# First unit of products between the token turns, memsets and small copies moved, at the beginning of a hybrid decoder step

## The chip, the cores and the metric

One Trainium2 chip, one of its cores. The metric is the time of one execution on the device in microseconds. The engines are TensorE (PE, matmul; PEld is its weight load), VectorE (DVE), ScalarE (ACT), GpSimd (POOL) and SyncE (SP), which issues most DMAs. TensorE's clock has two levels, 1.2 and 2.4 GHz; the profile writes the granted clock as a share of full speed.

## The reference, cut to what matters

One layer of a decoder trunk for 512 prompt tokens and 32 sample tokens, 544 columns in all, width 1024. Every sub-layer has an RMSNorm in front and behind. The change touches the beginning of the first sub-layer:

```python
hp = rms_norm(y_p, g_mix_pre[l])          # x * rsqrt(mean(x^2) + eps) * g
proj = hn @ w_in                          # 1024 -> 2048: q, k, v (512 each), u (512)
# S5 on u: diagonal complex scan, 32 groups of 16 channels, 64 states each
dt = jnp.exp(log_dt)[:, None]
lam_bar = jnp.exp(lam * dt)
b_bar = ((lam_bar - 1.0) / lam)[..., None] * lax.complex(b_re, b_im)
bu = jnp.einsum("btgh,gph->btgp", uf, b_bar)
_, h = lax.associative_scan(combine, (a, bu), axis=1)
y = jnp.real(jnp.einsum("btgp,ghp->btgh", h, c)) + d_skip * uf
```

Behind it come differential attention, a GLU, an output projection, a cross-attention into 256 memory tokens and a SwiGLU FFN. They are not changed.

## The kernel before

Every large product is made in three parts of reduced precision: weights and activations are split into a high part (`w_hi`, `x_hi`, a rounding copy on ACT) and a low part (`w_lo`, `x_lo`, a subtraction on DVE or POOL), and PE adds hi x hi, hi x lo and lo x hi in PSUM. Features lie on the partitions, the 544 token columns are two halves of 272. Weights come in units of 1 MB (`w_raw`, two slots; 8 feature tiles x 256 columns): SP loads unit n when `w_lo` of unit n-2 is made, ACT makes `w_hi` (L702), DVE makes `w_lo` (`split_lo`, L1141). Unit n gives the output tiles j = 2n and 2n+1, each 8 x 3 x 2 = 48 matmuls (L1806 in `product`). The accumulator of tile j is a pair of banks that depends on j mod 2 (`acc`), so `product` waits with `acc_out >= j - 1` until tile j-2 has been moved out by ACT.

The beginning, line by line. SP loads the tokens (`x_nat`), `ident`, `ones` (L466), the first weight unit and the parameters of the scan. POOL zeroes `c_out` and `c_pad`, waits for the scaled tokens, and zeroes `b_pad` (L634). ACT and DVE take the sums of squares, the roots, and scale the tokens into `xs` (L794, L1195). PE turns the rows of small parameters and of `log_dt` (L1843); DVE copies the first into `par`, halves four columns of it (L1199) and copies the second (L1202). ACT makes `w_hi` of unit 0. PE then turns the tokens, feature tile by feature tile: five transposes a tile (L1862, four of 128 tokens and one of 32) into the banks `X_BANKS`; ACT makes `x_hi` (L799) and DVE `x_lo` (L1206) of each tile, straight from PSUM.

After that every engine walks the same hand-written list `order` and does its share of each entry, in its own queue. Its start is `par, main 0, mats_c, main 1, mats_b 0, main 2, mats_b 1, main 3, fir, main 4, s5s 0`.

- `par`: the scan's parameters. ACT: exponential of dt (L820), `w_hi` of unit 1 (`hi_ahead(1)`), exponential of the two `lam_dots` (L823), and once DVE has the arguments (`p_arg`), tanh and two sines (L825 to L827, a table load between them). DVE: `lam_dots` (L1241), the lambda scalars, the arguments (to L1268), `split_lo` of unit 1, and with the sines a long row of small operations (from L1272), `split_lo` of unit 2 (44.57 us in the rows below), the copies of the turned `c` into `c_pad` and `c_sgn` (L1340, L1341), and `b_pad`.
- `main n`: PE multiplies unit n; ACT moves its two tiles out (units 0 and 1 into `uT`, L811) and makes `w_hi` of unit n+2.
- `mats_c`: PE turns the start states and `c` (10 transposes); DVE makes `split_lo` of unit 3, `c_out`, and zeroes `fir` (L1396).
- `mats_b n`: PE turns one of the two matrices of `b_pad`, 16 transposes; the first has `keep_busy(bank(4), 10)` in front, matmuls on `ident` without a use (L1830), two per call. The second waits for all four copies of the first (`bT_out`). ACT copies them into `b_in` (L832). DVE makes `rot` and two low parts.

In ACT's queue `par` thus stands ahead of the evacuation of unit 0, and PE's second unit waits for that evacuation:

```python
            if first and j >= 2:
                e.wait_ge(acc_out, j - 1)
```

Of the kernel before, what the change touches and what calls it, by code (L numbers as in the profile page):

```python
# [80 lines left out]
def build(nc, A, O):  # L81
# [79 lines left out]
    b_pad = at("b_pad", [P, 2, CH, SF, P], F32, C0 + 8704)  # L161
    st_nat = at("st_nat", [P, 2, P], F32, C0 + 27648)
# [5 lines left out]
    x_nat = at("x_nat", [P, 5, D], F32, C0)  # L168
# [197 lines left out]
    X_BANKS = (4, 6, 2, 0, 4, 6, 4, 6)  # L366
# [10 lines left out]
    order = [("par", 0), ("main", 0), ("mats_c", 0), ("main", 1), ("mats_b", 0), ("main", 2), ("mats_b", 1), ("main", 3),  # L377
# [69 lines left out]
    def _(sp_eng):  # L447
# [16 lines left out]
        e.dma_start(x_nat[0:NS_TOK, 4, :], A["x_sample"].rearrange("b t d -> (b t) d")).then_inc(x_in, 16)  # L464
# [155 lines left out]
    def _(pool):  # L620
# [64 lines left out]
    def _(act):  # L685
# [95 lines left out]
        e.wait_ge(S("eps_ready"), 1)  # L781
        e.activation(small[:, 60:61], small[:, EPS_COL:EPS_COL + 1], ACT.Sqrt)
        for t in SQ_ACT:
            rows = P if t < 4 else NS_TOK
            e.wait_ge(*((S(f"x_in{t}"), 16) if t < 4 else (x_in, 16)))
            e.activation(xs[0:rows, t, :], x_nat[0:rows, t, :], ACT.Square, accum_out=small[0:rows, t:t + 1]).then_inc(S("x_ss"), 1)
        e.wait_ge(S("x_ms"), 2)
# [14 lines left out]
        for kind, n in order:  # L802
            if kind == "m7":
                evac(14 + n, two(vT[:, 2 + n, :]))
            elif kind == "main":
# [10 lines left out]
                hi_ahead(min(n + 2, U_GLU))  # L816
            elif kind == "par":
# [3 lines left out]
                hi_ahead(1)  # L821
# [5 lines left out]
                e.activation(sp[:, 6], sp[:, 3], ACT.Sin, scale=0.5).then_inc(S("p_funcs"), 1)  # L827
            elif kind == "mats_b":

                for d in range(CH):  # L830
                    e.wait_ge(S("bT_full"), CH * n + d + 1)
                    e.activation(b_in[:, :, n, d, :], bank(4 + d).rearrange("p (a b) -> p a b", a=SF), ACT.Copy)\  # L832
                        .then_inc(S("bT_out"), 1)
            elif kind == "fir":
                e.wait_ge(S("fir_full"), 1)
# [93 lines left out]
            elif kind == "mem_a":  # L929
# [4 lines left out]
                e.wait_ge(S("x_ms"), 2 + 1)  # L934
# [189 lines left out]
    def _(dve):  # L1124
# [54 lines left out]
        e.memset(small[:, EPS_COL:EPS_COL + 1], EPS).then_inc(S("eps_ready"), 1)  # L1179
# [7 lines left out]
        e.tensor_scalar(small[:, 8:12], small[:, 0:4], 1.0 / D, EPS, ALU.mult, ALU.add).then_inc(S("x_ms"), 1)  # L1187
        e.tensor_scalar(small[0:NS_TOK, 12:13], small[0:NS_TOK, 4:5], 1.0 / D, EPS, ALU.mult, ALU.add).then_inc(S("x_ms"), 1)
# [47 lines left out]
        for kind, n in order:  # L1236
            if kind == "par":
# [31 lines left out]
                split_lo()  # L1269
# [1111 lines left out]
```

## Time and profile before

| what | us |
|---|---|
| median of three runs (all: 981.1, 981.74, 985.83) | 981.74 |
| the profiled execution, its own time | 980.58 |
| its span, first to last instruction | 978.8 |
| PE busy in the span | 934.9 |
| DVE, ACT, POOL busy | 438.3, 357.2, 198.8 |
| mean granted clock of TensorE | 0.992 |

Read the start first: the list of slices of the page shows PE at three tenths in the first fortieth of the span (24.5 us) and at nine tenths from the second on. The busy share says nothing of the speed: the matmuls of the first unit are busy at a lower clock as well. Times in the rows are microseconds from the start of the span; a row of the timeline merges like instructions and gives the start of the first, the time from there to the end of the last, and how many there are.

### The profile page before, as it was taken

The page shows a single profiled execution, that of the slowest core. Times are in us where ns is not written, and L with a number is a line of the kernel's source. Part 1 is how long each engine was busy: PE and PEld are TensorE (multiplying, and loading weights), DVE is VectorE, ACT ScalarE, POOL GpSimd, SP SyncE. Part 2 cuts the span into 40 slices and gives each one's busy share as a digit, 9 for nine tenths or more (in the row PEclk, how much of TensorE's full clock was granted, in tenths as well). Part 3 has the DMA queues.
Part 4 walks back from the last instruction along what each step waited for, and adds up shares of the span by engine and source line. Part 5 has one row for each costly group of instructions (what it writes and reads, how often), then busy time and mean ns, then how long its engine had stood idle before and what let it go on. Part 6 is the DMA issues. An engine that isn't in the chain of part 4 may idle for free.

```text
span 978.8 us, 17712 instructions
## 1 busy us (share of the span) xinstructions
PE 934.9 (96%) x7526; PEld 863.0 (88%) x7526; DVE 438.3 (45%) x876; ACT 357.2 (36%) x560; POOL 198.8 (20%) x66
## 2 busy tenths in 40 slices
PE   3999999889899999999989999999999999999997
PEld 2999998765799889976569899999999999999996
DVE  5799974565445696121644662222222222001103
ACT  5432223665454473145425542222222222222111
POOL 3000000202100033200110003333333333343330
PEclk9999999999999999999999989999999999999999
DMA  7314205432342359268142011222222222222212
GB/s 209 110 40 131 85 4 191 149 116 87 117 148 64 112 181 330 90 249 310 40 133 86 2 44 47 92 93 92 93 94 90 86 86 75 87 76 76 86 33 92
DMA packets 81247, 105.84 MB, mean 108 GB/s; under 512 B 9473, under 2 KB 64642, under 8 KB 81058
## 3 DMA queue, kind: packets, MB, share of 16 engines
q1 hardware_dynamic: 80960, 104.92, 32.3%
q8 instruction: 46, 0.75, 0.3%
q14 instruction: 15, 0.12, 0.0%
q10 hardware_dynamic: 226, 0.05, 0.0%
HBM read 98.26 MB, written 6.70 MB: 107 GB/s over the span
## 4 chain that ended last, share of the span: by engine, by line
PE 87%; DVE 5%; ACT 4%; issue 2%; DMA 1%; ACTq 0%; DVEq 0%; POOL 0%
PE pall L1806 59%; PE pall L1818 7%; PE pall L2128 4%; PE pall L1843 3%; PE pall L2179 1%; PE pall L1830 1%; PE pall L2198 1%; PE pall L2004 1%; PE pall L1879 1%; PE pall L2234 1%; PE pall L1996 1%; PE pall L1896 1%; PE pall L1862 1%; PE pall L1900 1%; DVE a_s L1464 1%
## 5 line engine op out<-in xcount | busy, mean ns | idle before, releaser
L628 POOL TENSOR_TENSOR w_lo<-w_raw,w_hi 128x2048 fp32r<-128x2048 f32 (+1 forms) x38 | 170.3, 4483 | 462.4 <-ACT w_hi L702 380.3
L1806 PE MATMUL pall<-x_hi,w_hi 128*128 128x272 f32 x1024 | 214.0, 291 | 0.5 <-issue 0.5
L1806 PE MATMUL pall<-x_lo,w_hi 128*128 128x272 f32 x1024 | 212.6, 289 | 0.0
L1806 PE MATMUL pall<-x_hi,w_lo 128*128 128x272 f32 x1024 | 211.2, 288 | 0.0
L1806 PEld LDWEIGHTS pall<-x_hi,w_hi 128*128 128x128 f32 x1024 | 161.0, 189 | 1.4 <-issue 0.7
L1806 PEld LDWEIGHTS pall<-x_lo,w_hi 128*128 128x128 f32 x1024 | 162.0, 190 | 0.0
L1806 PEld LDWEIGHTS pall<-x_hi,w_lo 128*128 128x128 f32 x1024 | 161.2, 189 | 0.0
L702 ACT ACTIVATE w_hi<-w_raw 128x2048 fp32r<-128x2048 f32 (+1 forms) x61 | 114.9, 1883 | 106.6 <-PE pall L1806 91.9
L1806 PE MATMUL pall<-g_hi,w_hi 128*128 128x272 f32 x352 | 73.2, 289 | 0.0
L1806 PE MATMUL pall<-g_lo,w_hi 128*128 128x272 f32 x352 | 72.8, 288 | 0.0
L1806 PE MATMUL pall<-g_hi,w_lo 128*128 128x272 f32 x352 | 72.7, 288 | 0.0
L1141 DVE TENSOR_TENSOR w_lo<-w_raw,w_hi 128x2048 fp32r<-128x2048 f32 x23 | 52.7, 2290 | 10.8 <-ACT w_hi L702 10.7
L1135 DVE TENSOR_TENSOR sq<-pall,rstd 128x544 f32<-128x544 f32 (+1 forms) x24 | 16.3, 677 | 91.7 <-PE pall L1806 87.8
L1806 PEld LDWEIGHTS pall<-g_lo,w_hi 128*128 128x128 f32 x352 | 55.4, 189 | 0.0
L1806 PEld LDWEIGHTS pall<-g_hi,w_hi 128*128 128x128 f32 x352 | 55.2, 189 | 0.0
L1806 PEld LDWEIGHTS pall<-g_hi,w_lo 128*128 128x128 f32 x352 | 55.1, 189 | 0.0
L1135 DVE TENSOR_TENSOR tt<-pall,rstd 128x544 f32<-128x544 f32 (+1 forms) x24 | 16.1, 676 | 83.6 <-PE pall L1806 80.4
L1103 ACT ACTIVATE g_hi<-sq 128x544 f32 x20 | 13.2, 659 | 98.1 <-DVE sq L1135 98.1
L1138 DVE TENSOR_TENSOR sqacc<-sqacc,sq 128x544 f32<-128x544 f32 x12 | 11.3, 941 | 76.3 <-ACT sq L735 76.3
L1099 ACT ACTIVATE tt<-tt 128x544 f32<-128x544 f32 x20 | 13.2, 659 | 79.3 <-DVE tt L1135 79.3
L1818 PE MATMUL pall<-x_hi,w_hi 128*128 128x272 f32 x128 | 37.4, 292 | 0.7 <-DVE x_lo L1141 0.7
L1818 PE MATMUL pall<-x_hi,w_lo 128*128 128x272 f32 x128 | 37.0, 289 | 0.0
(383 smaller groups left out, 1582.5 us busy)
## 6 DMA issues: line engine op xcount, KB each, us to landing
w_raw<-in_w_gate SPq DMA_DIRECT2D x10, 1024.0 KB, 5.3
w_raw<-in_w_up SPq DMA_DIRECT2D x10, 1024.0 KB, 5.3
w_raw<-in_w_in SPq DMA_DIRECT2D x8, 1024.0 KB, 6.9
w_raw<-in_w_down SPq DMA_DIRECT2D x8, 1024.0 KB, 5.2
dm_kv<-in_cache_mem_v SPq DMA_DIRECT2D x5, 1024.0 KB, 13.8
w_raw<-in_w_out SPq DMA_DIRECT2D x4, 1024.0 KB, 8.3
d_k<-in_cache_k SPq DMA_DIRECT2D x16, 256.0 KB, 3.3
d_v<-in_cache_v SPq DMA_DIRECT2D x16, 256.0 KB, 4.2
```

Source lines behind the costliest of these rows:

```text
L628: e.tensor_tensor(w_lo[:, n % 2, 0:w], w_raw[:, n % 2, 0:w], w_hi[:, n % 2, 0:w].bitcast(F32), ALU.subtract)\
L702: e.activation(w_hi[:, n % 2, 0:w], w_raw[:, n % 2, 0:w], ACT.Copy).then_inc(w_hi_ready, 1)
L1099: e.activation(tt[:, m, :], tt[:, m, :], ACT.Silu).then_inc(S("silu"), 1)
L1103: e.activation(g_hi[:, bass.ds(i * 2 + (m + 2), 1), :], sq[:, m:m + 1, :], ACT.Copy).then_inc(S("g_hi_ready"), 1)
L1135: return e.tensor_tensor(out, a, b, ALU.mult)
L1138: return e.tensor_tensor(out, a, b, ALU.add)
L1141: return e.tensor_tensor(out, a, b, ALU.subtract)
L1464: ins = e.tensor_tensor_reduce(out=a_s[:, n % 2, c, 0:nk], in0=bank(c)[:, 0:nk], in1=alibi[:, h, ALIBI_W - nk:ALIBI_W], scale=1.0, scalar=NEG,
L1806: ins = mm(acc(j)[:, a, :], w, x[:, k_x + k, a * HALF:(a + 1) * HALF], start=first and k == 0 and s_, stop=last and k == kts - 1 and t_)
L1818: ins = mm(out[:, 0:HALF], w, x[:, k, in_half(a)], start=k == 0 and s_, stop=k == KT - 1 and t_)
L1843: ins = e.transpose(dst[0:src.shape[1], at_:at_ + w], src, ident[0:w, 0:w])
L2128: ins = mm(bank(2 * (pr % 2) + t), x[:, 4 * part + k, rows], w[:, n % 2, w_cols], start=part == 0 and k == 0 and i == 0, stop=part == 1 an ...
```

## The change

The tokens of the samples get a tile of their own (`xs_nat`), so that `b_pad` and `st_nat` can lie elsewhere; `b_pad` is zeroed right behind `c_out`, `c_pad` after three low parts. PE runs `keep_busy` twice before the first turn. `w_hi` and `w_lo` of unit 0 are made in two halves, the second halves between the tiles 1 and 2 of the tokens. The eight turns of tokens use two pairs of banks in alternation; from the third on a turn stands between the products of the tiles before (`first_unit`). `w_hi` of unit 1 is made before tile 6 of `x_hi`; `split_lo` of unit 1 goes from the middle of `par` to right behind the last low part of the tokens. The copies into `c_pad` and `c_sgn` and the zeroing of `fir` go from DVE to ACT. `mats_b 0` stands behind main 2, directly in front of `mats_b 1`, whose banks now wait one by one; `w_hi` of unit 4 is made behind it. Some semaphores are merged (`eps_ready` and `x_ms` into `x_eps_ms`).

```diff
     st = at("st", [P, 2, P], F32, C0 + 94208)
-    b_pad = at("b_pad", [P, 2, CH, SF, P], F32, C0 + 8704)
-    st_nat = at("st_nat", [P, 2, P], F32, C0 + 27648)
+    b_pad = at("b_pad", [P, 2, CH, SF, P], F32, C0 + 19968)
+    st_nat = at("st_nat", [P, 2, P], F32, C0 + 17408)
     st_end = [at("st_end0", [P, P], F32, C0 + 95232), at("st_end1", [P, P], F32, Y0 + 16896)]
...
-    x_nat = at("x_nat", [P, 5, D], F32, C0)
+    x_nat = at("x_nat", [P, 4, D], F32, C0)
+    xs_nat = at("xs_nat", [P, D], F32, TMP)
     xs = at("xs", [P, 5, D], F32, C0 + 45056)
...
     XS_ACT, XS_DVE = (0, 4), (1, 2, 3)
-    X_BANKS = (4, 6, 2, 0, 4, 6, 4, 6)
-    order = [("par", 0), ("main", 0), ("mats_c", 0), ("main", 1), ("mats_b", 0), ("main", 2), ("mats_b", 1), ("main", 3),
+    X_BANKS = (4, 6) * (KT // 2)
+    order = [("par", 0), ("main", 0), ("mats_c", 0), ("main", 1), ("main", 2), ("mats_b", 0), ("mats_b", 1), ("main", 3),
              ("fir", 0), ("main", 4), ("s5s", 0), ("main", 5), ("s5s", 1), ("main", 6), ("s5y", 0), ("s5s", 2), ("m7", 0),
...
         e.memset(c_out[:], 0.0).then_inc(S("zeroed"), 1)
+        e.memset(b_pad[:], 0.0).then_inc(S("zeroed"), 1)
+        e.wait_ge(S("xs_lo"), 3)
         e.memset(c_pad[:], 0.0).then_inc(S("zeroed"), 1)
-        e.wait_ge(S("xs_ready"), 5)
-        e.memset(b_pad[:], 0.0).then_inc(S("zeroed"), 1)
         e.wait_ge(S("s5_y"), SF)
...
             rows = P if t < 4 else NS_TOK
-        hi_ahead(0)
+        def first_hi(half):
+            cols = slice(half * 1024, (half + 1) * 1024)
+            ins = e.activation(w_hi[:, 0, cols], w_raw[:, 0, cols], ACT.Copy)
+            ins.then_inc(w_hi_ready, 1) if half else ins.then_inc(S("xs_hi"), 1)
+        e.wait_ge(w_loaded[0], 16)
+        todo[0] = 1
+        first_hi(0)
         e.wait_ge(S("par_ready"), 1)
         for k in range(KT):
+            if k == 2:
+                first_hi(1)
+            elif k == 6:
+                hi_ahead(1)
             e.wait_ge(S("xsT_full"), k + 1)
...
                     evac(j, two(dst[:, t, :]), scale=HD ** -0.5 if dst is qT else 1.0)
-                hi_ahead(min(n + 2, U_GLU))
+                if n != 2:
+                    hi_ahead(min(n + 2, U_GLU))
             elif kind == "par":
...
                 e.activation(sp[:, 1], sp[:, 0], ACT.Exp).then_inc(S("p_funcs"), 1)
-                hi_ahead(1)
                 e.wait_ge(S("lam_dots"), 2)
...
                 e.activation(sp[:, 6], sp[:, 3], ACT.Sin, scale=0.5).then_inc(S("p_funcs"), 1)
+            elif kind == "mats_c":
+                e.wait_ge(S("zeroed"), 3)
+                for r in range(2):
+                    e.wait_ge(S("cT_full"), r + 1)
+                    for d in range(2):
+                        rows = slice(64 * d, 64 * d + 64)
+                        src = bank(4 + r)[rows, :].rearrange("p (f d h) -> p f d h", d=2, h=GH)[:, :, d, :]
+                        e.activation(c_pad[rows, :, r, 16 * d:16 * d + 16], src, ACT.Copy, scale=1.0 - 2.0 * r).then_inc(S("cT_out"), 1)
+                        e.activation(c_sgn[rows, r], src, ACT.Copy, scale=1.0 - 2.0 * r).then_inc(S("cT_out"), 1)
             elif kind == "mats_b":
...
                         .then_inc(S("bT_out"), 1)
+                if n:
+                    hi_ahead(4)
             elif kind == "fir":
+                e.wait_ge(S("c_out"), 4)
+                e.activation(fir[:].rearrange("p a b c -> p (a b) c"), ident[:].unsqueeze(1).broadcast_to([P, SF * CH, P]), ACT.Copy, scale=0.0)\
+                    .then_inc(S("fir_zero"), 1)
                 e.wait_ge(S("fir_full"), 1)
...
         e.tensor_copy(sp[:, 0], bank(2)[:, 0:CT_N]).then_inc(S("dtT_ready"), 1)
-        split_lo()
+        def first_lo(half):
+            e.wait_ge(*((w_hi_ready, 1) if half else (S("xs_hi"), 1)))
+            cols = slice(half * 1024, (half + 1) * 1024)
+            ins = sub(w_lo[:, 0, cols], w_raw[:, 0, cols], w_hi[:, 0, cols].bitcast(F32))
+            if half:
+                ins.then_inc(w_lo_ready, 1)
+        lo_done[0] = 1
+        first_lo(0)
         for k in range(KT):
-            e.wait_ge(S("xs_hi"), k + 1)
+            if k == 2:
+                first_lo(1)
+            e.wait_ge(S("xs_hi"), k + 2)
             e.scalar_tensor_tensor(out=x_lo[:, k, :], in0=banks(X_BANKS[k]), scalar=par[:, G_MIX_PRE + k:G_MIX_PRE + k + 1],
                                    in1=x_hi[:, k, :].bitcast(F32), op0=ALU.mult, op1=ALU.subtract).then_inc(S("xs_lo"), 1)
+        split_lo()
...
                 e.tensor_scalar(c(3), c(7), 3.1415925, -3.1415925, ALU.min, ALU.max).then_inc(S("p_arg"), 1)
-                split_lo()
                 e.wait_ge(S("p_funcs"), 2 + 3)
...
                 e.tensor_copy(st[:].rearrange("p a b -> p (a b)"), bank(6)[:, 0:2 * P]).then_inc(S("st_ready"), 1)
-                for r in range(2):
-                    e.wait_ge(S("cT_full"), r + 1)
-                    if r == 0:
-                        e.wait_ge(S("zeroed"), 2)
-                    for d in range(2):
-                        rows = slice(64 * d, 64 * d + 64)
-                        src = bank(4 + r)[rows, :].rearrange("p (f d h) -> p f d h", d=2, h=GH)[:, :, d, :]
-                        e.tensor_scalar(c_pad[rows, :, r, 16 * d:16 * d + 16], src, 1.0 - 2.0 * r, None, ALU.mult).then_inc(S("cT_out"), 1)
-                        e.tensor_scalar(c_sgn[rows, r], src, 1.0 - 2.0 * r, None, ALU.mult).then_inc(S("cT_out"), 1)
...
                         e.tensor_tensor(c_out[rows, :, r, :, 16 * g:16 * g + 16], t0[rows], t1[rows], op).then_inc(S("c_out"), 1)
-                e.wait_ge(S("c_out"), 4)
-                e.memset(fir[:], 0.0).then_inc(S("fir_zero"), 1)
             elif kind == "fir":
...
         e.wait_ge(consts_in, 32)
+        keep_busy(bank(6), 12)
         e.wait_ge(rows_in, 16 * N_ROW_LOADS)
...
         transposes(bank(2), [dt_rows[:].rearrange("p a b -> p (a b)")]).then_inc(S("dtT"), 1)
-        for k in range(KT):
-            if k == 0:
-                e.wait_ge(S("xs_ready"), 5)
-            if k in (2, 3):
-                e.wait_ge(*((S("par_ready"), 1) if k == 3 else (S("dtT_ready"), 1)))
-            if k >= 4:
-                e.wait_ge(S("xs_lo"), (1, 2, 5, 6)[k - 4])
+        keep_busy(bank(6), 8)
+        e.wait_ge(S("xs_ready"), 5)
+        def x_turn(k):
+            if k >= 2:
+                e.wait_ge(S("xs_lo"), k - 1)
             for t in range(5):
...
             ins.then_inc(S("xsT_full"), 1)
+        def first_product(m, k):
+            e.wait_ge(S("xs_lo"), k + 1)
+            if k == 4:
+                e.wait_ge(w_lo_ready, 1)
+            wcol = slice(k * 256 + m * P, k * 256 + (m + 1) * P)
+            wh, wl = w_hi[:, 0, wcol], w_lo[:, 0, wcol]
+            for w, x, s_, t_ in ((wh, x_hi, True, False), (wh, x_lo, False, False), (wl, x_hi, False, True)):
+                for a in range(2):
+                    ins = mm(acc(m)[:, a, :], w, x[:, k, a * HALF:(a + 1) * HALF], start=k == 0 and s_, stop=k == KT - 1 and t_)
+            return ins
+        def first_unit():
+            e.wait_ge(S("dtT_ready"), 1)
+            for k in range(KT - 2):
+                e.wait_ge(S("xs_lo"), k + 1)
+                x_turn(k + 2)
+                for m in range(2):
+                    first_product(m, k)
+            for m in range(2):
+                for k in (KT - 2, KT - 1):
+                    ins = first_product(m, k)
+                ins.then_inc(acc_full, 1)
+        x_turn(0)
+        x_turn(1)
...
             if kind == "main":
-                unit(n, J_W_IN + 2 * n, KT, 256, x_hi, x_lo, ready=(lambda k: (S("xs_lo"), max(4, k + 1))) if n == 0 else None)
+                if n == 0:
+                    first_unit()
+                else:
+                    unit(n, J_W_IN + 2 * n, KT, 256, x_hi, x_lo)
             elif kind == "m7":
...
                 e.wait_ge(S("st_ready"), 1)
-                if n:
-                    e.wait_ge(S("bT_out"), CH)
-                else:
+                if n == 0:
                     keep_busy(bank(4), 10)
...
                 for d in range(CH):
+                    if n:
+                        e.wait_ge(S("bT_out"), d + 1)
                     transposes(bank(4 + d), [b_pad[:, n, d, f, :] for f in range(SF)]).then_inc(S("bT_full"), 1)
```

## Rows read from the trace of the kernel before

**Rows 1.** Page, part 1: busy us of each engine, share, instructions

```profile
PE 934.9 (96%) x7526; PEld 863.0 (88%) x7526; DVE 438.3 (45%) x876; ACT 357.2 (36%) x560; POOL 198.8 (20%) x66
```

**Rows 2.** Chain of waits, 0 to 200 us: start us, us, what

```profile
14.48 3.50 DVE par L1199
...
22.03 0.72 ACT x_hi L799
22.77 0.80 DVE x_lo L1206
...
26.26 14.12 PE pall L1806 x96
40.37 1.09 PE pall L1843 x10
41.46 12.04 PE pall L1806 x96
53.50 2.23 PE pall L1830 x20
```

**Rows 3.** Timeline, 0 to 62 us: start us, us, engine line op, what, count

```profile
3.64 0.45 SPq L466 DMA_DIRECT2D ones<-in_t_ones  x1
...
14.44 3.52 POOL L634 MEMSET b_pad<- 128x4096 f32 x1 [9.30 <-ACT xs L794]
...
29.98 0.62 PE L1806 MATMUL pall<-x_hi,w_lo 128*128 128x272 f32 x2
...
30.43 0.41 PE L1806 MATMUL pall<-x_hi,w_hi 128*128 128x272 f32 x2
...
30.68 0.42 PE L1806 MATMUL pall<-x_lo,w_hi 128*128 128x272 f32 x2
```

**Rows 4.** Timeline of PE, 11 to 27 us

```profile
18.06 5.22 PE L1862 MATMUL pall<-ident,xs 128*128 128x128 f32 x20 [0.98 <-DVE sp L1202]
```

**Rows 5.** DMA issues, 0 to 12 us: count, KB, us to landing

```profile
ones<-in_t_ones SPq DMA_DIRECT2D x1, 64.0 KB, 6.9
```

**Rows 6.** Timeline of PE, 286 to 300 us, turns at 2.4 GHz

```profile
294.28 0.77 PE L1970 MATMUL pall<-ident,x_res 128*128 128x128 f32 x5
294.98 0.66 PE L1843 MATMUL pall<-ident,mem_nat 128*128 128x128 f32 x4
```

**Rows 7.** Timeline, 0 to 62 us, the parameters of the scan

```profile
27.74 0.22 DVE L1241 CUSTOM_DVE_ANT_0 lamp<-lamv 128x64 f32<-128x64 f32 x1
...
30.24 0.19 ACT L823 ACTIVATE small<-small 128x2 f32<-128x2 f32 x1
...
30.46 0.16 DVE L1141 TENSOR_TENSOR small<-small 128x1 f32<-128x1 f32 x1 [2.30 <-ACT small L823]
...
32.71 0.17 DVE L1268 TENSOR_SCALAR sp<-sp 128x16 f32<-128x16 f32 x1
32.79 2.29 DVE L1141 TENSOR_TENSOR w_lo<-w_raw,w_hi 128x2048 fp32r<-128x2048 f32 x1
...
34.67 1.18 ACT L811 ACTIVATE uT<-pall 128x544 f32<-128x544 f32 x1
...
35.00 0.17 DVE L1272 TENSOR_SCALAR sp<-sp 128x16 f32<-128x16 f32 x1
```

**Rows 8.** Timeline of PE at 196 us, then stretches: busy us, clock, DMA, GB/s

```profile
196.27 2.43 PE L2101 MATMUL pall<-ident,small 68*128 68x68 f32 x16 [2.43 <-DVE small L1533]
...
198.00:199.00 1.00, 1.00 (x7) 1.00 (x7) 0.00 (x0) 0.00 (x0) 0.00 (x0) 0.50 0.96 345
559.00:560.00 1.00, 0.68 (x3) 0.69 (x4) 1.00 (x4) 1.00 (x3) 0.00 (x0) 0.75 0.00 0
568.00:569.00 1.00, 1.00 (x6) 1.00 (x6) 1.00 (x4) 0.84 (x2) 0.00 (x0) 0.50 0.00 0
```

**Rows 9.** Timeline of DVE, 36 to 75 us

```profile
44.57 2.29 DVE L1141 TENSOR_TENSOR w_lo<-w_raw,w_hi 128x2048 fp32r<-128x2048 f32 x1
...
72.51 1.76 DVE L1396 MEMSET fir<- 128x2048 f32 x1 [0.49 <-DVE c_out L1394]
```

More of the change, by code:

```diff
@@ L463, in _ @@
             e.dma_start(x_nat[:, t, :], x_view[:, t, :]).then_inc(S(f"x_in{t}"), 16)
-        e.dma_start(x_nat[0:NS_TOK, 4, :], A["x_sample"].rearrange("b t d -> (b t) d")).then_inc(x_in, 16)
+        e.dma_start(xs_nat[0:NS_TOK, :], A["x_sample"].rearrange("b t d -> (b t) d")).then_inc(x_in, 16)
         e.dma_start(ident[:], A["t_ident"]).then_inc(consts_in, 16)
@@ L780, in _ @@
         e.dma_start(dt2[:], A["ssm_log_dt"][0].rearrange("(c g) -> c g", g=2)).then_inc(rows_in, 16)
-        e.wait_ge(S("eps_ready"), 1)
+        e.wait_ge(S("x_eps_ms"), 1)
         e.activation(small[:, 60:61], small[:, EPS_COL:EPS_COL + 1], ACT.Sqrt)
@@ L785, in _ @@
             e.wait_ge(*((S(f"x_in{t}"), 16) if t < 4 else (x_in, 16)))
-            e.activation(xs[0:rows, t, :], x_nat[0:rows, t, :], ACT.Square, accum_out=small[0:rows, t:t + 1]).then_inc(S("x_ss"), 1)
-        e.wait_ge(S("x_ms"), 2)
+            e.activation(xs[0:rows, t, :], x_nat[:, t, :] if t < 4 else xs_nat[0:rows, :], ACT.Square, accum_out=small[0:rows, t:t + 1]).then_inc(S("x_ss"), 1)
+        e.wait_ge(S("x_eps_ms"), 3)
         e.activation(small[:, 8:12], small[:, 8:12], ACT.Sqrt)
@@ L793, in _ @@
             rows = P if t < 4 else NS_TOK
-            e.activation(xs[0:rows, t, :], x_nat[0:rows, t, :], ACT.Copy, scale=small[0:rows, 16 + t:17 + t]).then_inc(S("xs_ready"), 1)
-        hi_ahead(0)
+            e.activation(xs[0:rows, t, :], x_nat[:, t, :] if t < 4 else xs_nat[0:rows, :], ACT.Copy, scale=small[0:rows, 16 + t:17 + t])\
+                .then_inc(S("xs_ready"), 1)
+        def first_hi(half):
[5 more added lines that the diff above has]
+        first_hi(0)
         e.wait_ge(S("par_ready"), 1)
         for k in range(KT):
+            if k == 2:
+                first_hi(1)
+            elif k == 6:
+                hi_ahead(1)
             e.wait_ge(S("xsT_full"), k + 1)
@@ L933, in _ @@
                     e.activation(mem_sq[:, t, :], mem_nat[:, t, :], ACT.Square, accum_out=small[:, t:t + 1]).then_inc(S("x_ss"), 1)
-                e.wait_ge(S("x_ms"), 2 + 1)
+                e.wait_ge(S("x_eps_ms"), 3 + 1)
                 e.activation(small[:, 8:10], small[:, 8:10], ACT.Sqrt).then_inc(S("x_root"), 1)
@@ L1177, in split_lo @@
             lo_done[0] += 1
-        e.memset(small[:, EPS_COL:EPS_COL + 1], EPS).then_inc(S("eps_ready"), 1)
+        e.memset(small[:, EPS_COL:EPS_COL + 1], EPS).then_inc(S("x_eps_ms"), 1)
         for t in SQ_DVE:
@@ L1186, in _ @@
         e.wait_ge(S("x_ss"), 5)
-        e.tensor_scalar(small[:, 8:12], small[:, 0:4], 1.0 / D, EPS, ALU.mult, ALU.add).then_inc(S("x_ms"), 1)
-        e.tensor_scalar(small[0:NS_TOK, 12:13], small[0:NS_TOK, 4:5], 1.0 / D, EPS, ALU.mult, ALU.add).then_inc(S("x_ms"), 1)
+        e.tensor_scalar(small[:, 8:12], small[:, 0:4], 1.0 / D, EPS, ALU.mult, ALU.add).then_inc(S("x_eps_ms"), 1)
+        e.tensor_scalar(small[0:NS_TOK, 12:13], small[0:NS_TOK, 4:5], 1.0 / D, EPS, ALU.mult, ALU.add).then_inc(S("x_eps_ms"), 1)
         e.wait_ge(S("x_root"), 1)
@@ L1542, in _ @@
                 e.wait_ge(S("x_ss"), 5 + 2)
-                e.tensor_scalar(small[:, 8:10], small[:, 0:2], 1.0 / D, EPS, ALU.mult, ALU.add).then_inc(S("x_ms"), 1)
+                e.tensor_scalar(small[:, 8:10], small[:, 0:2], 1.0 / D, EPS, ALU.mult, ALU.add).then_inc(S("x_eps_ms"), 1)
                 e.wait_ge(S("x_root"), 1 + 1)
```

## The prediction

> **What bounds the kernel now.** I read the page first: TensorE (PE) is busy for 934.9 us of a span of 978.8 us [rows 1]. Only what moves PE's queue of work can change the time, so the next view is the chain of waits over the start [rows 2]. It shows 3.50 us in which `par` on VectorE (DVE) alone is what everybody waits for, then the token turns, and from 26.26 us on PE without a break: the first unit of products (14.12 us for 96 matmuls), the ten turns of `mats_c` at 40.37, and the second unit at 41.46 us (12.04 us for as many). From there PE goes on through `keep_busy` (53.50) and the later units. I therefore measure the change at one point: **when the second unit starts, 41.46 us now**. The order `mats_b` moves in is neutral for PE if nobody is late, so whatever is won or lost there reaches the end.
>
> The all-engine timeline shows two reasons for the slow start [rows 3]. `par` on DVE takes 3.50 us for four columns, and it starts and ends with GpSimd's (POOL's) memset of `b_pad` (14.44 to 17.96 us). And the products run at two speeds: from 29.98 to 30.43 us is 0.45 us a pair, from 30.43 to 30.68 it is 0.25 us. The first spacing is 272 columns each at 1.2 GHz, the second belongs to 2.4 GHz; the clock rose at about 30.3 us. 20 turns in 5.22 us [rows 4] are part of the eight microseconds of turns before the products, which had not raised it; the products had run 4.0 us when it rose.
>
> **The change, part by part.**
>
> *Memsets.* `b_pad` is zeroed right behind `c_out`, a tile of the same size: two times 3.52 us from 0.7 us on, until 7.8 us, when DVE waits for tokens anyway. `par` then costs what its neighbours of this size do, about 0.2 us, and 3.3 us go from the chain. The Trainium skill (SBUF — State Buffer, "Who interferes with whom") says that GpSimd and a VectorE instruction that uses both ports exclude each other for a whole instruction; by that rule, too, the wait is gone, and the `c_pad` memset, now behind three low parts, could hold DVE up once more. It has a quarter of `b_pad`'s columns, so 0.9 us at most, between two low parts that PE wants 2.2 us apart: I take 0, and 0.9 as the upper end.
>
> *Warming.* Ten `keep_busy` calls are 20 matmuls in 2.23 us, 0.111 us each at 2.4 GHz [rows 2]; at 1.2 GHz I take twice that, 0.22 us. The 12 + 8 calls are 40 matmuls: 4.5 us if all warm, 8.9 us if none. They can start when `ones` has landed, 3.64 [rows 3] + 6.9 = 10.5 us [rows 5]. With the clock rising 4.0 us after, as now: 18 matmuls at 0.22 (to 14.5), 6 at 0.111, the two parameter turns (0.3), 16 at 0.111: 17.2 us. The bounds are 15.3 (all warm) and 20.0 us (none).
>
> *First unit between the turns.* A warm turn of one feature tile takes 0.70 us (294.28 to 294.98) [rows 6]. Turns 0 and 1 end at 17.9 and 18.6; `x_hi` 0.72 and `x_lo` 0.80 [rows 2] put the first low part at P0 = 19.4 us. Then six steps of one turn and twelve matmuls, 0.70 + 12 x 0.125 (12.04 us / 96) = 2.20 us, and 3.0 us for the last two tiles: the unit ends at P0 + 16.2 = 35.6 us and `mats_c` at 36.7, against 41.46. **On PE that is 4.8 us won.** The half-unit splits on ScalarE (ACT) and DVE are the same columns in two pieces and lie beside PE. `w_hi` of unit 1, before tile 6, is covered: tile 6 is turned only four steps after P0.
>
> *What is behind it in the queues.* The second unit may not overwrite the first accumulator before ACT has moved it to `uT`. In ACT's queue that evacuation stands behind `par`: exponentials, tanh, sines, each waiting for DVE. Now this is over in time [rows 7]: `lam_dots` on DVE at 27.74, exponential on ACT, arguments 30.46 to 32.88, table load and sines, `uT` 34.67 to 35.85, 5.6 us before PE wants it. In the changed kernel DVE's low parts are stretched over the unit, and `split_lo` of unit 1 has been put between the last low part and `lam_dots`. The last low part is at T7 = P0 + 5 x 2.20 + 0.70 + 0.72 + 0.80 = 32.6 us. Behind it: `w_lo` 2.29, `lam_dots` 0.35 (two like 0.22, one behind the other), exponential and its hand-over 0.2, arguments 2.42, from there to the end of `uT` 2.97 (32.88 to 35.85): 8.25 us. **The second unit starts at 32.6 + 8.25 = 40.9 us**, not 36.7. The win of 4.8 us shrinks to 0.6, with PE idle for 4.2 us.
>
> *The clock in that gap.* The rows for a fallen clock [rows 8]: after 2.43 us idle before 196.27 the clock was 0.50 in 198 to 199; and it was low from 559 to 569 us, 10 us long, where PE had had some gaps of up to 1 us. So 4.2 us idle most probably costs a new rise, 4.0 us at half speed = 2.0 us lost; ends 0 (it holds) and 5 us (as at 559). I take 2.0, by the one rise under products. The Trainium skill (TensorE: Matmul & The Clock Gate, "Why this matters for your kernels") says that idle gaps between bursts of matmuls put the engine back to its low clock; the fall at 196 us agrees, and by the rule rival 1 below has little.
>
> *Moved from DVE to ACT.* Eight small copies for `c_pad` and `c_sgn`, and the zeroing of `fir` (1.76 us on DVE) [rows 9]. On ACT the copies stand between `w_hi` of unit 2 and the next evacuation, the zeroing behind main 3, where the unit's 12 us hold only about 5 us of ACT's work. If that cover were gone they would cost their own length, some 4 and 2 us; here 0. DVE's later work is not late: behind the sines it has 9.6 us to its next `w_lo` (35.00 to 44.57) [rows 7, 9], so `w_lo` of unit 2 is ready near 39.7 + 9.6 + 2.3 = 51.6 us, and main 2 wants it at 53 or later. 1.3 us of slack, tied to the same event.
>
> *`mats_b` behind the third unit.* The same 20 + 32 instructions. In the second matrix each bank waits for its own copy on ACT, which began with the first bank of the first matrix, while PE was at its other three: 0, and at most the last copy's half microsecond. `w_hi` of unit 4 stands behind both and is wanted only after main 3.
>
> Sum: -0.6 + 2.0 = **+1.4 us**, so 980.58 + 1.4 = 982.0 us for the profiled execution; the median of the runs shown stands 1.2 us above that execution, so I forecast 983.2 us.
>
> **Rivals.**
> 1. *The same wait, but the clock holds through the gap.* For it: gaps of about 1 us in the token stage don't count here, and PE comes out of 20 dense microseconds. Against: 2.43 us was enough at 196. 981.74 - 0.6 = 981.1 us.
> 2. *The win is kept.* ACT's `par` part is done sooner than I add up, and the second unit starts at 36.7: 981.74 - 4.8 = 977.0 us. Against it is the order of the two queues in the diff; the chain would have to shrink from 8.25 to 4 us.
> 3. *The low clock through the start (slower).* The place is the stretch from 10.5 us to T7, and what decides is P0: the second unit starts at P0 + 21.45, so above P0 = 20.0 us the change loses, one for one. If the 40 warming matmuls all run at 1.2 GHz, they and the parameter turns end at 20.0, turns take 1.29 us [rows 4], P0 = 22.8; one first step at 1.2 GHz (1.29 + 2.72 = 4.0 us), the rest warm: 37.8 = T7, 46.1 us for the second unit, +4.6, and +2.0 behind the gap: 988.3 us. If the clock stays down through the unit, T7 is 45.6 and the sum +14, 996 us. For it: the eight microseconds of turns that did not raise it, and 559 to 569. Against: `keep_busy` is matmuls, not turns. The Trainium skill (TensorE: Matmul & The Clock Gate, "Part 4: PE-mode transpose") says that a transpose doesn't count as TensorE being busy in the same way; the low stretch from 18.06 us agrees, and mixing turns into the unit speaks against this change by it.
> 4. *The change does not do what it says*, that is, the products don't run between the turns: the loop is written out, I give it nothing of its own.
>
> **How the numbers follow.** Forecast 0.48 (981.5 to 984.5, up to 987 with a long low clock), rival 1 0.20 (980 to 982), rival 2 0.09 (976.5 to 978.5), rival 3 0.23 (985 to 996, most of it under 990). The three runs before spread from 981.1 to 985.83 us, so about 0.5% is what a measurement can tell from no change: 976.8 to 986.6. The range from 979.5 to 989.5 leaves out rival 2 and the far half of rival 3. Faster by over 0.5% needs more than the whole win: 0.05. Slower: most of rival 3 and the long low clock of the forecast, 0.22. Same: 0.73.
>
> **What the changed profile would show.** `par` at 0.2 us; 40 matmuls of `keep_busy` from 10.5 us; turns and products alternating every 2.2 us; the first unit ending near 36 us. Right or wrong is decided by one row: the first pair of the second unit, idle before it for about 4 us, released by ACT's `uT` at 40 to 42 us; and by the spacing of pairs behind it, 0.46 or 0.25 us. The forecast is wrong if that unit starts by 38 us, or after 43, or if PE waits at main 2 or main 3 for `w_lo`.

## The result and the profile after

The changed kernel takes 984.85 us in the median of 22 runs (979.75 to 989.54), the kernel before 980.97 us in 22 runs beside it (976.74 to 985.94). The ratio is 1.0038 with a 95% interval of 1.0022 to 1.0053: 0.4% slower, clear of noise, and within the 0.5% that the prediction called no change. The profiled execution took 988.83 us with a span of 987.0 us; it is one of the longer ones, and why it is so much longer is a part of the answer below. The work of each engine on its page:

```profile
PE 943.3 (96%) x7566; PEld 870.5 (88%) x7566; DVE 432.2 (44%) x868; ACT 361.7 (37%) x570; POOL 198.5 (20%) x66
```

PE is busy 8.4 us longer than in [rows 1] with only 40 matmuls of `keep_busy` more. These 40 are not the reason: up to the start of the second unit PE is busy 26.3 us in the kernel before and 26.8 us in the changed one, since turns and products at the full clock make up for the 7.0 us of `keep_busy`. The other 8 us lie behind it, in work that is the same. There PE did the same work more slowly.

The chain of waits over the start of the changed kernel (start us, us, what), which answers to [rows 2]:

```profile
10.45 4.98 PE pall L1860 x24
...
17.66 0.62 PE pall L1893 x5
...
19.11 0.80 DVE x_lo L1248
...
20.85 1.71 PE pall L1906 x12
22.55 0.61 PE pall L1893 x5
...
33.22 0.79 DVE x_lo L1248
34.00 2.20 DVE w_lo L1171
...
39.44 1.28 ACT L841
...
41.06 0.99 ACT uT L826
...
42.18 25.77 PE pall L1836 x192
...
73.67 12.03 PE pall L1836 x96
```

Nearly every step that the prediction wrote down is a row here. `keep_busy` starts at 10.45 us, the first turn at 17.66, the first low part ends at 19.91, turns (0.61) and products (1.71) alternate every 2.31 us, the last low part ends at 34.01. And then PE is not in the chain for 8.2 us: `w_lo` of unit 1, the exponential for `lam_dots`, the arguments, the table load, the sines, `uT`. The second unit starts at **42.18 us, 0.7 us later than before**, although PE had finished the first one and `mats_c` at 38.24. The timeline of PE around it, against the spacings of [rows 3]:

```profile
37.20 1.04 PE L1873 MATMUL pall<-ident,c_nat 128*128 128x128 f32 x8
42.18 0.79 PE L1836 MATMUL pall<-x_hi,w_hi 128*128 128x272 f32 x2 [3.94 <-ACT uT L826]
42.77 0.66 PE L1836 MATMUL pall<-x_lo,w_hi 128*128 128x272 f32 x2
43.23 0.66 PE L1836 MATMUL pall<-x_hi,w_lo 128*128 128x272 f32 x2
...
45.48 0.41 PE L1836 MATMUL pall<-x_lo,w_hi 128*128 128x272 f32 x2
45.73 0.41 PE L1836 MATMUL pall<-x_hi,w_lo 128*128 128x272 f32 x2
```

PE was idle for 3.94 us, released by ACT's `uT`, and the pairs behind the gap are 0.46 us apart until about 45.5 us, then 0.25. The stretches show the same in the granted clock (us, then busy us of PE, PEld, DVE, ACT, POOL, the clock, DMA share, GB/s):

```profile
43.00:44.00 1.00, 1.00 (x6) 1.00 (x6) 0.83 (x6) 1.00 (x1) 0.00 (x0) 0.50 0.00 0
...
46.00:47.00 1.00, 1.00 (x11) 1.00 (x10) 0.86 (x8) 0.98 (x4) 0.00 (x0) 1.00 0.00 0
```

The low level of 0.50 is 1.2 GHz of 2.4; it lasts 3.4 us here. Units 1 and 2 together take 25.77 us. Without a gap ahead of them they take 24.06 (run 4 below), behind a gap through which the clock held 24.29 (run 2). So 1.7 us are lost behind the gap, 1.5 of them to the clock. From there on the two kernels run side by side: main 3 starts at 73.67 us, 2.4 us after the 71.3 before, and near 195 us the same instructions are still 2.35 us apart. That is what the changed part itself costs in these two executions. The remaining difference, 8.3 - 2.4 = 5.9 us, arises between 198 and 508 us, in code that is the same:

```profile
204.00:205.00 1.00, 1.00 (x6) 0.51 (x4) 0.00 (x0) 0.94 (x3) 0.00 (x0) 0.50 0.28 41
214.00:215.00 1.00, 1.00 (x3) 0.42 (x2) 0.96 (x5) 0.00 (x0) 0.00 (x0) 0.50 0.00 0
504.00:505.00 1.00, 0.53 (x2) 0.47 (x2) 0.38 (x1) 0.90 (x2) 0.00 (x0) 0.50 0.00 0
```

```profile
204.00:205.00 1.00, 1.00 (x11) 1.00 (x11) 0.66 (x2) 1.00 (x2) 0.00 (x0) 1.00 0.00 0
214.00:215.00 1.00, 1.00 (x11) 1.00 (x11) 0.97 (x5) 1.00 (x5) 0.00 (x0) 1.00 1.02 391
```

The first fence is the changed kernel, the second the kernel before. The changed one's profiled execution has four more low stretches of about 3.4 us in those stages than the one before (in 199 to 206, 212 to 217, 260 to 264 and 502 to 507 us; before there is one, in 197 to 202). Both have one of 10 us near 560 and one of 5 us at the end.

### The profile page after: what moved, and what is told of

Same layout as the page of the kernel before. It is cut to its first block, busy times and chain, and to the rows that moved or that the text cites. A ratio compares the mean times of both kernels' runs of the same rounds, so it can differ in the third digit from the quotient of the medians.

```text
span 987.0 us, 17800 instructions
## 1 busy us (share of the span) xinstructions
PE 943.3 (96%) x7566; PEld 870.5 (88%) x7566; DVE 432.2 (44%) x868; ACT 361.7 (37%) x570; POOL 198.5 (20%) x66
## 4 chain that ended last, share of the span: by engine, by line
PE 88%; DVE 5%; ACT 3%; issue 2%; DMA 1%; SPq 0%; DVEq 0%; POOL 0%; ACTq 0%
PE pall L1836 58%; PE pall L1848 7%; PE pall L2192 4%; PE pall L1873 3%; PE pall L1860 2%; PE pall L2243 2%; PE pall L2068 1%; PE pall L2262 1%; PE pall L2060 1%; PE pall L1906 1%; PE pall L1940 1%; PE pall L2298 1%; PE pall L1957 1%; DMA out_new_k_prompt<-k_tok 1%; DMA ones<-in_t_ones 1%
## 5 line engine op out<-in xcount | busy, mean ns | idle before, releaser
L1836 PE MATMUL pall<-x_hi,w_hi 128*128 128x272 f32 x992 | 207.0, 290 | 4.5 <-ACT uT L826 3.9
L1836 PE MATMUL pall<-x_lo,w_hi 128*128 128x272 f32 x992 | 205.5, 288 | 0.0
L1836 PE MATMUL pall<-x_hi,w_lo 128*128 128x272 f32 x992 | 204.3, 287 | 0.0
L1836 PEld LDWEIGHTS pall<-x_hi,w_hi 128*128 128x128 f32 x992 | 155.6, 189 | 5.5 <-issue 4.8
L1836 PEld LDWEIGHTS pall<-x_lo,w_hi 128*128 128x128 f32 x992 | 156.6, 189 | 0.0
L1836 PEld LDWEIGHTS pall<-x_hi,w_lo 128*128 128x128 f32 x992 | 155.8, 189 | 0.0
L1171 DVE TENSOR_TENSOR w_lo<-w_raw,w_hi 128x2048 fp32r<-128x2048 f32 (+1 forms) x24 | 52.8, 2201 | 15.0 <-ACT w_hi L703 14.7
L1860 PE MATMUL pall<-ident 128*128 128x128 f32 x230 | 32.4, 295 | 11.5 <-DMA ones<-in_t_ones 10.4
L1860 PEld LDWEIGHTS pall<-ident 128*128 128x128 f32 x230 | 29.6, 205 | 15.2 <-DMA ones<-in_t_ones 10.4
```

The costliest lines, as they stand in the source:

```text
L1171: return e.tensor_tensor(out, a, b, ALU.subtract)
L1836: ins = mm(acc(j)[:, a, :], w, x[:, k_x + k, a * HALF:(a + 1) * HALF], start=first and k == 0 and s_, stop=last and k == kts - 1 and t_)
L1860: mm(out[:, 0:P], ident[:], ident[:], start=True, stop=True)
```

## The experiments

Because low stretches come and go between executions, each run below is told with three numbers: where its second unit starts (one profiled execution), its median with the ratio to the kernel before, and the mean over its runs of span x (1 - mean granted clock), the clock's share, which is the time that the low clock took away at most, with the mean time less that. For the kernel before (89 runs beside these experiments) the mean, the share and the difference are 981.5 us, 9.4 and **972.1 us**; for the changed kernel (22 runs) 985.0, 12.2 and **972.8 us**. So of the 3.5 us between the means 0.7 us are left when the clock's share is taken out, as much as the later start of the second unit, and 2.8 us are clock: 1.7 behind the gap and 1.1 in later stages.

Three things limit these numbers. The runs scatter: a mean less the share is good to about 0.6 us with 12 runs, 0.5 with 22 and 0.2 with 89, and the share itself to 1 or 2 us (95%). So the 0.7 us stand just clear of noise and the 1.1 us do not. The place of the second unit comes from one execution: it moves with the landing of the constants and the length of the warming, by 1.25 us between the two executions of run 4, so 0.7 us between two traces would prove nothing by itself. And the record of the clock says 1.00 from the start of the span, also where the pairs of the kernel before are 0.45 us apart [rows 3]:

```profile
29.00:30.00 1.00, 1.00 (x7) 1.00 (x6) 0.00 (x0) 1.00 (x1) 0.00 (x0) 1.00 0.01 2
```

The low clock of the first unit is therefore not in the share but stays in the time less the share.

**1. The gap filled.** 17 calls of `keep_busy` where PE waits.

```diff
                 transposes(bank(4 + r), ...).then_inc(S("cT_full"), 1)
+                keep_busy(bank(7), 17)
```

> The changed kernel with 17 more keep_busy calls (34 matmuls of 0.111 us, 3.8 us) on PE behind mats_c, in the 3.94 us in which PE waited for ACT's uT. Queue theory: the second unit still starts at 42.2 us, since ACT's queue sets it, but its pairs are 0.25 us apart from the start, main 1 takes 12.0 instead of 13.7 us, and everything up to 190 us is 1.7 us earlier than in the changed kernel. Time about 983 us against 984.9 as far as the rest is alike. Rival (the clock falls by a schedule of its own, not by the gap): the pairs are 0.45 us apart for 3.4 us as in the changed kernel, no gain.

Timeline of PE:

```profile
38.17 3.96 PE L1860 MATMUL pall<-ident 128*128 128x128 f32 x34
42.28 0.49 PE L1836 MATMUL pall<-x_hi,w_hi 128*128 128x272 f32 x2 [0.15 <-ACT uT L826]
42.60 0.41 PE L1836 MATMUL pall<-x_lo,w_hi 128*128 128x272 f32 x2
42.85 0.42 PE L1836 MATMUL pall<-x_hi,w_lo 128*128 128x272 f32 x2
```

The second unit starts at 42.28 us as before the filling, and the pairs are 0.25 us apart from the second on. So the low clock at this place came from the gap: with it filled, the clock did not fall. The two units take 24.29 us and main 3 starts at 72.29, 1.4 us sooner than in the changed kernel, not 1.7. Median 980.75 us, ratio 0.9992 (0.9968 to 1.0016): 4.1 us less than the changed kernel where 1.7 were expected. Its clock share is 7.7 us against 12.2, so most of the rest is the clock of later stages, which came out well in these 12 runs; with the clock taken out it is 973.5 us, no better than the changed kernel. Useless matmuls in a wait bring back the speed, not the wait.

**2. One part undone: `split_lo` of unit 1 back in `par`.**

```diff
-        split_lo()
...
                 e.tensor_scalar(c(3), c(7), 3.1415925, ...).then_inc(S("p_arg"), 1)
+                split_lo()
                 e.wait_ge(S("p_funcs"), 2 + 3)
```

> The changed kernel with one part undone: split_lo of unit 1 stands again in the middle of par, behind the arguments, where DVE waits for the sines. Queue theory: 2.2 us leave the chain last low part, lam_dots, arguments, sines, uT; the second unit starts at 42.2 - 2.2 = 40.0 us, the gap shrinks from 3.9 to 1.7 us, and if the clock holds through it main 1 takes 12.0 us: 2.2 to 3.9 us faster than the changed kernel, 981 to 982.7 us. Rival (w_lo of unit 1 or the load of it sets the start): the second unit starts no earlier than 42.

Chain of waits:

```profile
40.27 24.29 PE pall L1836 x192
...
70.28 12.03 PE pall L1836 x96
```

The second unit starts at 40.27 us, 1.9 us earlier where the 2.20 us of one `w_lo` were expected: the exponential for dt on ACT, which starts behind the last `x_hi`, now stands in the chain in place of DVE's last low part and `lam_dots`, and it is 0.3 us longer than they are. `w_lo` of unit 1 was not what PE waited for. PE still waits 2.0 us for `uT`, and behind this shorter gap the two units take 24.29 us: the clock held. Median 981.43 us, 1.0006 (0.9982 to 1.0029); 971.2 us without the clock's share, 1.6 less than the changed kernel. The median alone would not have shown a gain over the kernel before.

**3. The sines behind the evacuation.** ACT moves unit 0 out first, then tanh and sines.

```diff
             elif kind == "par":
...
-                e.wait_ge(S("p_arg"), 2)
-                e.activation(sp[:, 4], sp[:, 2], ACT.Tanh, scale=0.5)...
...
# in main 0, behind the two evacuations, ahead of hi_ahead(2):
+                if n == 0:
+                    e.wait_ge(S("p_arg"), 2)
+                    e.activation(sp[:, 4], sp[:, 2], ACT.Tanh, scale=0.5)...
```

> The changed kernel with tanh and the two sines behind the evacuation of unit 0 on ACT, ahead of w_hi of unit 2; nothing moved on DVE. Queue theory: the second unit starts right behind mats_c at 38.2 us, no gap, warm, ends at 50.3. Then w_lo of unit 2 becomes late: DVE has it at 41.1 + 9.6 + 2.3 = 53.0 us, so PE waits 2.7 us at main 2, which starts at 53.0 instead of 55.9 us (with the low clock) in the changed kernel: 2.9 us faster as far as the clock holds, 982 us. Rival (the wait for uT is not what holds PE): the second unit starts at 41 or later.

Chain of waits:

```profile
51.03 2.30 DVE w_lo L1172
53.37 13.60 PE pall L1837 x96
...
72.70 12.03 PE pall L1837 x96
```

The wait for `uT` is gone, and the one that was hidden behind it is there: `w_lo` of unit 2 ends at 53.33 us and main 2 starts at 53.37, after 2.8 us of waiting. The clock fell in this gap too (13.60 us for a unit of 12.03). Median 984.29 us, 1.0026 (1.0004 to 1.0048). Expected was 982: the start of main 2 was right to 0.4 us, and what I had left open, the clock, took 1.6 us again. Without the clock's share it is 970.8 us.

**4. Sines behind, and `w_lo` of unit 2 ahead of them.** As 3, with `w_hi` of unit 2 ahead of the sines on ACT, and on DVE

```diff
+                split_lo()
                 e.wait_ge(S("p_funcs"), 2 + 3)
...
-                split_lo()
                 e.wait_ge(S("stT"), 1)
```

> As the run with the sines behind the evacuation, but w_hi of unit 2 ahead of the sines and w_lo of unit 2 on DVE before it waits for the sines. Queue theory: the second unit starts at 38.2 us, no wait at main 2 (w_lo ready at 42.5) nor main 3 (b_pad and w_lo of unit 3 at 62 to 65 us, wanted at 64 to 68): main 3 starts at 67.9 us against 73.7 in the changed kernel and 71.3 before: 5.8 us less than the changed kernel, 3.4 less than before, 977.5 us as far as the clock stays alike later. Rival (DVE's chain becomes the bound): b_pad is late, PE waits 1 to 3 us at mats_b or main 3, 979 to 981 us.

Chain of waits:

```profile
38.63 24.06 PE pall L1837 x192
...
68.41 12.03 PE pall L1837 x96
```

No gap from the first unit to main 3, which starts at 68.41 us against 73.67 in the changed kernel and 71.3 before. DVE's chain did not become the bound. The start is 0.4 us later than expected because the warming took that much longer in this execution. Median 979.11 us, 0.9976 (0.9950 to 1.0003), 968.5 us without the clock's share: 3.6 us less than before, where 3.4 were expected. The interval still touched 1, so it ran again:

> The run with the sines and w_lo of unit 2 moved, once more, for its interval. Second unit at 38.6 us, main 3 at 68.4 us, 979 us; ratio to the kernel before 0.9965 to 0.998 over both runs if its 2.9 us are real, 1.000 if the first reading was the clock's luck.

Chain of waits:

```profile
16.82 0.62 PE pall L1894 x5
...
37.38 24.06 PE pall L1837 x192
...
67.17 12.03 PE pall L1837 x96
```

978.77 us, 0.9969 (0.9946 to 0.9991), 968.6 us without the clock's share. In that profiled execution the constants landed 0.2 us sooner and the first `keep_busy` took 4.53 us instead of 5.49, so everything up to main 3 lies 1.2 us earlier. The low stretch near 195 us was half as long and the one of 10 us near 560 did not come, though one of 3.4 us at 491 did; it took 973.35 us. This is the version that is faster than the kernel before, by 0.2 to 0.3%, with the interval of the second reading clear of 1, and faster than the changed kernel by more.

**5. The memsets alone.** The kernel before with `b_pad` zeroed right behind `c_out`.

```diff
         e.memset(c_out[:], 0.0).then_inc(S("zeroed"), 1)
+        e.memset(b_pad[:], 0.0).then_inc(S("zeroed"), 1)
         e.memset(c_pad[:], 0.0).then_inc(S("zeroed"), 1)
-        e.wait_ge(S("xs_ready"), 5)
-        e.memset(b_pad[:], 0.0).then_inc(S("zeroed"), 1)
```

> The kernel before with one part of the change alone: b_pad zeroed right behind c_out (with the addresses and the sample tokens' own tile that this needs), c_pad behind it. Port theory: par takes 0.2 instead of 3.5 us, the turns from the third on, the products (at 1.2 GHz for 4 us as before), the parameters and the second unit are all 3.3 us earlier, the second unit at 38.2 us with no wait for uT: 977.8 us against 981.1. Rival (the 3.5 us were DVE's own or only hid another wait, such as w_lo of unit 0): the second unit starts at 40 to 41.5.

Timeline, then the chain of waits:

```profile
14.52 7.79 PE L1862 MATMUL pall<-ident,xs 128*128 128x128 f32 x30 [2.48 <-ACT xs L794]
14.56 0.17 DVE L1199 TENSOR_SCALAR par<-par 128x4 f32<-128x4 f32 x1
...
30.37 0.45 PE L1806 MATMUL pall<-x_hi,w_lo 128*128 128x272 f32 x2
30.65 0.41 PE L1806 MATMUL pall<-x_hi,w_hi 128*128 128x272 f32 x2
```

```profile
25.28 14.56 PE pall L1806 x96
...
40.93 12.03 PE pall L1806 x96
```

`par` fell from 3.50 to 0.17 us, as expected, and it brought 1.0 us, not 3.3: the products start at 25.28 instead of 26.26. The reason is the first row: the turns now follow one another, the first six without a break, at 1.2 GHz, 1.3 us each (7.79 / 6), and eight of them are over 10 us. Of the 3.3 us two thirds lay beside turns that PE had to make anyway; PE had idled for only 0.98 us [rows 4]. The clock rose at about 30.4 us, the same moment as in the kernel before [rows 3] and so 1.0 us later into the unit. That makes the unit 14.56 us long instead of 14.12, and the second unit starts 0.5 us earlier, at 40.93. Median 979.24 us, 0.9974 (0.9955 to 0.9993); without the clock's share 971.9, a mere 0.2 less than before, and the 0.5 us of the trace is within the noise of that number. The clock's share was 6.8 us in these 12 runs, 2.7 below the kernel before, so most of the measured gain stands in the clock of stages that are the same in both. That the memset does not change the clock there is assumed; the trace shows its 0.5 us and nothing more.

**6. All turns ahead of the products, warm.** Run 5 plus the two `keep_busy` and the place of `mats_b` as in the changed kernel; turns, low parts and parameters in their old order.

> The run with the memsets alone, plus keep_busy 12 and 8 and mats_b behind the third unit as in the changed kernel, but all turns ahead of all products as before, and the low parts and the parameters in their old order. Queue theory: products start near 24.5 us, warm, end at 36.5; the last low part is at 26 us instead of 34, so the parameters are over in time; the second unit starts at 37.5 us without a gap: 4 us less than before, 977 us, and less than the run with the sines behind. Rival (interleaving is worth its place): turns and low parts take longer than that, the second unit starts after 38.6 us.

Chain of waits:

```profile
19.10 3.77 DVE x_lo L1209 x5
...
24.51 12.24 PE pall L1809 x96
...
37.84 24.06 PE pall L1809 x192
```

The products start at 24.51 us, as expected, the second unit at 37.84 without a gap. Counted from the first turn (17.64 here, 18.06 and 16.82 in the two readings of run 4) it comes after 20.2 us, in run 4 after 20.6 both times. Interleaving is therefore not worth its place here: with warm turns it moves the first product forward from 24.5 to 20.9 us and spreads the low parts to 34 us, and these are what the scan's parameters and the second unit stand behind. Median 979.40 us, 0.9986 (0.9965 to 1.0007), 968.3 us without the clock's share: alike with run 4. The interval of the ratio still holds 1, so the gain over the kernel before rests on the number without the clock's share.

**7. Without the warming.** The changed kernel without its two `keep_busy` calls at the start.

> The changed kernel without the two keep_busy calls ahead of the turns. If the clock needs the warming: turns at 1.29 us, the first products from 17.5 us at 0.45 us a pair for about 4 us, then warm; last low part at 32.6 instead of 34.0, second unit at 40.8, some 1.4 us better than the changed kernel: the warming costs more at the front (turns wait until 17.5 us for it) than it brings. Rival (the interleaved unit does not raise the clock, since turns stand in it): the pairs stay at 0.45 us, the unit ends after 45 us, the second unit starts at 50 or later.

Chain of waits:

```profile
14.28 1.37 PE pall L1891 x5
...
18.74 3.02 PE pall L1904 x12
...
42.04 26.56 PE pall L1836 x192
```

A miss of 1.2 us in where the second unit starts, 42.04 and not 40.8: I had let the clock rise within one step, but it rose about 8 us after the first turn, 4 us after the first product (18.74 to 22.85), and two turns between the products were slow as well. So the warming is worth nothing for the start of the second unit (42.18 with it): it makes the turns begin 3.4 us later and gives that back. The rival is out, since an interleaved unit does raise the clock. The low stretch at the gap was longer here, 6.8 us from 40.3 us on, while PE was still idle (26.56 us for the two units). Median 983.30 us, 1.0022 (1.0004 to 1.0039), 972.3 without the clock's share.

**8. The memset late again.** The changed kernel with `b_pad` zeroed at its old moment, behind the scaled tokens (and `c_pad` ahead of it again).

> The changed kernel with the memset of b_pad at its old moment, behind the scaled tokens (14.4 to 17.9 us). Old step of the prediction (the memset is worth 3.3 us wherever it stands): the first low part and all behind it come 3.3 us later, the second unit at 45.5 us, 988 us. Theory from the run with the memsets alone (what stands behind par counts): in the changed kernel the first turned tile is only there at 18.3 us, when par is just done, so low parts and the second unit come at most 0.3 us later, 42.2 to 42.5, and the time is that of the changed kernel.

Timeline, then the chain of waits:

```profile
14.98 3.52 POOL L635 MEMSET b_pad<- 128x4096 f32 x1 [9.84 <-ACT xs L795]
...
16.03 2.50 DVE L1229 TENSOR_SCALAR par<-par 128x4 f32<-128x4 f32 x1
...
18.56 1.40 ACT L814 ACTIVATE x_hi<-pall,par 128x544 fp32r<-128x544 f32 x2 [2.69 <-DVE par L1229]
```

```profile
42.35 25.83 PE pall L1836 x192
```

DVE is held again (2.50 us for the four columns, until POOL ends), and the second unit starts at 42.35 instead of 42.18 us. Median 984.90 us, 1.0034 (1.0015 to 1.0052), the changed kernel's time. What a held engine costs is read from who waits for it: here the first turned tile is only there at about 18.3 us and `par` at 18.53, so 0.2 us are lost.

**9. A pure shift.** The kernel before with 32 more matmuls of `keep_busy` at `mats_b 0` (`keep_busy(bank(4), 26)`), 3.57 us by its chain (5.80 against 2.23).

> The kernel before with keep_busy 26 instead of 10 at mats_b 0: 32 more matmuls, PE 3.56 us later from 57 us on and nothing else changed. If later stages only move along: 981.1 + 3.6 = 984.6 us and the low stretches of the clock at the same places, shifted. Rival (where the clock falls later depends on the moment at which a stage begins): the time differs from 984.6 by more than 1 us, and the list of low stretches differs.

One of its stretches (columns as above):

```profile
217.00:218.00 1.00, 1.00 (x3) 0.61 (x2) 0.90 (x7) 0.00 (x0) 0.00 (x0) 0.50 0.00 0
```

Median 985.58 us over 8 runs, 1.0039 (1.0016 to 1.0062); 975.0 us without the clock's share, 2.9 more than before for 3.6 of work. Its profiled execution, 991.43 us, has low stretches at 201 to 209, 215 to 219, 263 to 267 and 505 to 509 us: the places of the changed kernel's, moved by 2 to 3 us, in a kernel that has nothing of the change. (Its parameters had landed 1.3 us late in that execution, so its second unit started at 42.45 us; it is a shift of 4.5 us by main 3, not of 3.6.) But its mean share of the clock is 10.2 us, hardly above the 9.4 of the kernel before. The forecast time was missed by 1.0 us, just at the bound that was set, and does not decide. So such stretches come without the change; that a shift by itself makes them more frequent is not shown by eight runs.

## Why the prediction was right

The forecast was 983.2 us, +1.4 us, by a wait that takes the place of the win. The mechanism came as written and the time lies 1.7 us above the forecast, but the change itself is +3.9 us in the medians and not +1.4: one term had the wrong sign, and a part of the time was in no term. Point by point:

- *The wait.* Right. The second unit waits for `uT`, released by ACT, for 3.94 us (forecast 4.2), and starts at 42.18 (40.9). Runs 2, 3 and 4 show that the queue order makes it: take `w_lo` out of the chain and the unit starts 1.9 us earlier, take the sines out and it starts right behind `mats_c`.
- *The start itself was 1.3 us too early in the sum*, by small terms: the warming ended 0.5 us later, so the first low part is at 19.9 instead of 19.4; the turn behind it cost 0.3 us more than the others; and each of the five steps is 2.31 us and not 2.20. By the starts in the timeline below a turn is 0.70 us, as forecast, and the twelve matmuls 1.61 instead of 1.50: the first pair behind a turn takes 0.36 us where the others take 0.25. The chain behind the last low part was 8.17 us for a forecast of 8.25. So the change loses 0.7 us at this point instead of winning 0.6.

```profile
22.39 0.77 PE L1893 MATMUL pall<-ident,xs 128*128 128x128 f32 x5
23.09 0.52 PE L1906 MATMUL pall<-x_hi,w_hi 128*128 128x272 f32 x2
23.45 0.41 PE L1906 MATMUL pall<-x_lo,w_hi 128*128 128x272 f32 x2
```

- *The clock in the gap.* Right: it fell, 1.7 us lost behind the gap (1.5 by the clock alone) for 2.0 forecast; run 1 shows the cause. Rival 1 (it holds) is out at 3.94 us; it is what happened in run 2 at 2.0 us.
- *Rival 2*, the win kept, is what run 4 is: 3.6 us without the clock's share. It needed moves in two queues that the change does not have.
- *Rival 3*, the low clock through the start, did not come: the forty matmuls raised it after about 4.5 us, and turns between products did not lower it. (Its turn of 1.29 us is 1.30 by [rows 4], 5.22 / 4, which changes nothing.) *Rival 4* is out by the chain, where turns and products alternate.
- *The memsets.* This step failed in size: "3.3 us go from the chain". Run 5 measured 1.0 us at the first product and 0.5 at the second unit, run 8 0.2 us in the changed kernel. The chain named DVE for 3.50 us, but PE behind it had idled only 0.98 us. It did no harm to the forecast, because the sum takes its start from the end of the warming and has no term of 3.3 us.
- *The sum.* +1.4 forecast, +3.5 in the means (+3.9 in the medians): +0.7 instead of -0.6 at the start, +1.7 instead of +2.0 behind the gap, and +1.1 of clock in later stages that the sum had nothing for. Whether the change causes that last part or it is the chance of 22 runs stays open. `w_lo` of unit 2 was ready at 52.96 us, 1.4 later than forecast like the event it hangs on, and PE came for it at 55.9; `mats_b` and the copies on ACT cost nothing: main 3 comes 2.4 us after its old moment, 0.7 + 1.7, with nothing in between.

## What to carry to other kernels

When work is spread so that one engine finishes sooner, write down what stands behind the last spread piece in every other engine's queue: here TensorE won 3.2 us (done at 38.24 against 41.46) and then waited 3.94 for what stood behind the last low part, 1.9 of them for one `w_lo` (run 2). Taking a wait away shows the next one (run 3), so follow the queue to the first point at which nothing is late. A wait that the chain names can lie beside work that the bounding engine has to do anyway (run 5): its price is the idle time of that engine behind it. And where the clock moves by itself, compare time less the clock's share, or a fixed event of several traces, before believing a change of 0.3%.

## What the runs showed of the hardware

The same kernel's executions differ by the number of low stretches: over 89 runs of the kernel before, the five with a mean granted clock of 0.997 took 976.4 to 978.1 us and the ten with 0.985 took 985.6 to 987.6 us. In the traces here the clock held through a gap of PE of 2.0 us (run 2) and was low behind gaps of 2.4 [rows 8], 2.8 and 3.9 us (run 3, the changed kernel); these are four places, not a threshold. The low level behind the gap of the changed kernel lasted 3.4 us, at the same gap in run 7 about twice that, and near 560 us it lasts 10 us in ten of the twelve profiled executions, which costs each of these at most 5 us. Turns between products neither kept the clock from rising (run 7) nor lowered it once it was up (the changed kernel). A memset on GpSimd held a four-column instruction of VectorE until the memset ended, twice (3.50 and 2.50 us), but not a copy out of PSUM that ran beside it (0.26 us at 15.73 in run 8). The Trainium skill (SBUF — State Buffer, "Who interferes with whom") has both as a rule, and the traces agree.
